# GpSimd's order in a Mamba-2 scan: both exponent additions of the next item ahead of the off-chunk addition

## The reference

```python
seg = cs[:, :, :, None] - cs[:, :, None, :]
lmat = jnp.exp(jnp.where(tri, seg, -jnp.inf))
cb = jnp.einsum('bclgn,bcsgn->bclsg', cc, bc)
y_diag = jnp.einsum('bclsge,bcsgep->bclgep', cb[..., None] * lmat, xdt)
...
y_off = jnp.einsum('bclgn,bcgepn,bclge->bclgep', cc, s_prev, jnp.exp(cs))
return (y_diag + y_off).reshape(b, L, H, P), s_last.reshape(b, H, P, N)
...
y = y_f + y_b[:, ::-1] + d_skip.astype(jnp.float32)[:, None] * xs.astype(jnp.float32)
y = y.reshape(b, L, D_INNER) * jax.nn.silu(z.astype(jnp.float32))
y = rmsnorm(y, g_norm).astype(h.dtype)
```

## Time and profile before

| | |
|---|---|
| time, median of 3 runs | 2935.42 us (2929.05 to 2936.62) |
| span of the profiled execution | 2938.1 us |
| instructions | 47237 |
| PE busy | 2839.0 us, 97% of the span |
| DVE busy | 1724.5 us, 59% |
| ACT busy | 1093.6 us, 37% |
| POOL busy | 260.0 us, 9% |
| part of the span in which items 4 to 19 are worked on | from about 2197 to 2322 us |

### The profile page before, as it was taken

The page is one execution under the profiler, slowest core; times in us unless marked ns, Lnnn a source line. Parts: engine busy times, 40 slices in busy tenths (PEclk is TensorE's granted clock), DMA queues, the critical chain, the costliest instruction groups (busy, mean ns, idle before and its releaser), DMA issues.

```text
span 2938.1 us, 47237 instructions
## 1 busy us (share of the span) xinstructions
PE 2839.0 (97%) x19482; PEld 2689.6 (92%) x19482; DVE 1724.5 (59%) x2584; ACT 1093.6 (37%) x1739; POOL 260.0 (9%) x201
## 2 busy tenths in 40 slices
PE   8999999998799999999999999999989999999998
PEld 6999999986589999999999999999945798999998
DVE  4667666647766655657565536467768747332334
ACT  4111126446865111146211126653324446211124
POOL 0000003000020000011000002000048511000002
PEclk8999999999999999999999999999989999999999
DMA  5445444520044444443443324622221133322233
GB/s 230 138 156 180 152 151 134 159 67 24 23 137 144 149 141 134 151 151 122 163 150 126 115 98 135 186 87 78 67 74 33 58 102 121 115 84 67 73 99 124
DMA packets 102631, 345.21 MB, mean 117 GB/s; under 512 B 10769, under 2 KB 27537, under 8 KB 100881
## 3 DMA queue, kind: packets, MB, share of 16 engines
q1 hardware_dynamic: 96786, 333.15, 34.9%
q10 hardware_dynamic: 5632, 9.05, 0.9%
HBM read 331.54 MB, written 10.62 MB: 116 GB/s over the span
## 4 chain that ended last, share of the span: by engine, by line
PE 83%; DVE 5%; ACT 4%; issue 3%; POOL 2%; DMA 1%; ACTq 0%; DVEq 0%; SPq 0%; POOLq 0%
PE P L1806 78%; ACT pb L946 1%; POOL mraw L707 1%; DVE wl L1187 1%; PE P L1865 1%; POOL toff L711 1%; DMA raw<-wgu_d 1%; DVE xl L1230 0%; DVE st L1320 0%; PE P L2009 0%; PE P L1724 0%; DVE xs L1494 0%; PE P L1750 0%; DVE toff L1529 0%; ACT pb L955 0%
## 5 line engine op out<-in xcount | busy, mean ns | idle before, releaser
L1806 PE MATMUL P<-xh,wh 128*128 128x320 f32 x4016 | 1006.0, 313 | 15.2 <-DVE xl L1230 7.9
L1806 PE MATMUL P<-xl,wh 128*128 128x320 f32 x4016 | 994.0, 310 | 0.0
L1806 PE MATMUL P<-xh,wl 128*128 128x320 f32 x4016 | 993.9, 310 | 0.0
L790 ACT CAST wh<-raw 128x1024 fp32r<-128x1024 f32 (+1 forms) x421 | 471.7, 1121 | 967.7 <-PE P L1806 806.8
L1806 PEld LDWEIGHTS P<-xh,wh 128*128 128x128 f32 x4016 | 693.9, 189 | 33.5 <-issue 14.6
L1187 DVE TENSOR_TENSOR wl<-raw,wh 128x1024 fp32r<-128x1024 f32 (+1 forms) x421 | 552.7, 1313 | 288.5 <-ACT wh L790 288.3
L1806 PEld LDWEIGHTS P<-xl,wh 128*128 128x128 f32 x4016 | 694.3, 189 | 1.2 <-issue 0.4
L1806 PEld LDWEIGHTS P<-xh,wl 128*128 128x128 f32 x4016 | 694.0, 189 | 0.0
L1806 PE MATMUL P<-hh,wh 128*128 128x320 f32 x1408 | 379.4, 310 | 0.0
L1806 PE MATMUL P<-hl,wh 128*128 128x320 f32 x1408 | 377.0, 308 | 0.0
L1806 PE MATMUL P<-hh,wl 128*128 128x320 f32 x1408 | 377.0, 308 | 0.0
(11 more groups left out here) (260 smaller groups left out, 2350.2 us busy)
## 6 DMA issues: line engine op xcount, KB each, us to landing
raw<-wgu_d SPq DMA_DIRECT2D x206, 512.0 KB, 3.7
mraw<-wmod_d SPq DMA_DIRECT2D x128, 512.0 KB, 3.6
raw<-wdB_d SPq DMA_DIRECT2D x64, 704.0 KB, 4.1
raw<-wdA_d SPq DMA_DIRECT2D x32, 704.0 KB, 5.5
raw<-ain_d SPq DMA_DIRECT2D x28, 512.0 KB, 3.6
raw<-sz_d SPq DMA_DIRECT2D x26, 512.0 KB, 3.8
raw<-sx_d SPq DMA_DIRECT2D x24, 512.0 KB, 3.6
raw<-aout_d SPq DMA_DIRECT2D x16, 512.0 KB, 3.6
```

What stands on the lines that cost most here:

```text
L790: nc.scalar.copy(wh[:, u.u % SPLITS, 0:n], raw[:, u.u % 2, 0:n]).then_inc(hi_done, 1)
L1806: ins = nc.tensor.matmul(P[:, u.banks[i], 0:C], w[:, u.u % SPLITS, k * 128:(k + 1) * 128], m[:, k, C * h:C * h + C], start=(k == 0 and w i ...
```

## The change

Within GpSimd's `scan`, `both(nxt, 1)` is issued ahead of `offs(nxt)` where it was issued behind it. For items of chunk 0, which have no `offs`, the order is as it was. No instruction, buffer or semaphore is added or removed, and the other engines' streams are the same.

```diff
                     if nxt < len(ITEMS):
                         both(nxt, 0)
+                        both(nxt, 1)
                         if ITEMS[nxt][0]:
                             offs(nxt)
-                        both(nxt, 1)
                     if i >= 1:
                         squares(i - 1)
```

## The result

The changed kernel takes 2940.95 us (median of 13 runs, 2936.19 to 2945.24), the kernel before 2935.42 us (13 runs, 2928.95 to 2937.99). The ratio is 1.0022, with a 95% interval of 1.0014 to 1.0030: 0.22% slower, some 4 to 9 us. That is a small loss, clear of the measurement's noise. The forecast was 2940.6.

The account below looks back on a forecast made before the run. Scan pace bound by a loop through POOL, DVE and ACT, PE just behind. Terms 4.2 - .3 + 2.1 + .55 - 1.3 = +5.2 us: span 2938.1 to 2943.3, median 2.7 lower, 2940.6; 8 in 10 range 2931.5 to 2947.

Parts of the forecast that it names:

- The lock: DVE's decay product meets `offs`, ends at E (end of the item's second addition) + 1.79; .46 us delay per item with state.
- A step with `blocks`: Steps into items 6, 8, 10, 12, 14, 16: POOL waits for ACT's exponential; 9.00 against 8.31 us, +4.2 in all.
- Plain steps: Steps into items 7, 11, 15, without `blocks` or `btok`: 7.70 against 7.84 us, -.3 in all.
- Steps with `btok` and into 17: Into 9 and 13, POOL's addition starts .16 us ahead of L1499: 8.70, +2.1 together; into 17 8.22, +.55.
- rival B: L1499 goes ahead of POOL's next addition into 9, 13 and 17, each .95 us shorter: +2.3, 2937.7 us; chance .20.
- The last chunk: Steps into items 18 and 19, without states or L1467: 6.6 and 6.1 against 7.25 and 6.72 us, -1.3 for both.
- Items 4 and 5: Start of the reordered items: item 5 keeps its pace, since POOL had spare time there; no term in the sum.
- Behind item 19: After the last item nothing changes: output, splits and first projection follow L1499 at the same distance; no term in the sum.
- what queues behind the new wait: `offs`, squares and `blocks` stand behind the second addition's wait for ACT; only POOL's own chain feels it, priced in the steps.
- Rival C: PE's longer `btok` wait, some 2.1 us, lowers the clock; three chunks lose up to 2.5 us each: 2948.1 us; chance .12.
- Rival A: The loop gains 1.24 us a step until PE's idle time is used up: -6, 2929.4 us; chance .10.

Follow-up runs that it names:

- e3: Changed kernel, with the scan's decay product reading the PSUM sum in place of the old state (its decay left out); 1.0004 of the time before.
- e1: Changed kernel with a second buffer for the second exponential, one for each half; 1.0019 of the time before.
- e9: Changed kernel with two buffers for the second exponential and ACT's square behind the exponentials, profiled once more; 1.0001 of the time before.
- e2: Changed kernel with ACT's second pair of exponentials ahead of its square of the output, one buffer kept; 1.0004 of the time before.
- e10: Changed kernel with POOL's first addition of items 5, 7, 9 and so on waiting until L1499 is ready; 2934.41 us, 1.0008 of before.

## Why the prediction was right

The time (2940.95 against 2940.6) and the sign were right; what counts is whether the terms were.

- *The lock*, that is, a DVE product of two SBUF operands waiting until the POOL operation under way ends. Right. L1467 ends at E + 1.78 (forecast 1.79), L1499 is ready at E + 3.57 (3.57). e3 shows the cause by taking it away.
- *A step with `blocks`, six times.* L700 starts at E + 3.40 (3.41), L1499 ends at E + 5.84 (5.86), the first addition at E + 6.98 (7.02), the second starts at E + 7.69 (7.73). The step is 8.98 against 9.00. The sum of the six is +4.4 with the one of 9.31, against +4.2. The reason given, that the old order hid ACT's turn-round on the one buffer, is only half of it: e1 shows that the buffer alone gives .15, and e9 against e2 that it gives .75 once ACT's square no longer stands in the way. Two waits of almost the same length lie on top of each other, and the text named one.
- *Plain steps, three times.* 7.70, 7.69 and 7.96 against 7.70; they give nothing in place of -.3. The third follows the fall of the clock. And the forecast took 7.84 as the old length of all three, where the one into item 7 was 7.66.
- *Steps with `btok` and into 17.* 8.71 and 8.21 against 8.70 and 8.22, +2.6 against +2.65. L1499 lost the race in all of them; rival B is out, and e10 confirms its price (.97 against .95).
- *The last chunk.* 6.56 and 6.03 against 6.6 and 6.1; -1.4 against -1.3.
- *Items 4 and 5* were taken as unchanged; from E of item 3 to E of item 5 it is .62 less. The clock was below 1.00 in this stretch in both kernels, so how much of it is the change's is open.
- *Behind item 19* was put at nothing, since "nothing is changed" there. That was wrong: +.90, for `offs` of item 19 now stands ahead of the squares that ACT's last square waits for. The passage on what queues behind the new wait had these squares done "a whole step earlier"; behind item 19 there is no further step. The last chunk gains .5 net, not 1.3.
- *Rival C, the clock,* was priced at up to 2.5 us a chunk, with no row behind that figure, and put at .12. It came true in part: PE's wait grew to 2.0 (forecast 2.1), the clock fell once in two such waits, and it cost .6 us (.3 in each of two steps), since PE isn't the engine that sets the pace. The wait was forecast well, but its length alone doesn't decide: 1.53 us was followed by a fall in e3 and 1.97 wasn't. The price was four times too high.
- *Rival A, PE as the bound,* did not come about in the changed kernel. The window of its chunk (item 9's `toff` to item 13's), for the earlier trace rows:

```profile
2232.10:2266.46 34.36, 30.66 (x212) 18.42 (x212) 30.74 (x45) 13.81 (x25) 27.39 (x25) 1.00 0.11 32
```

PE worked as much as before (30.66 against 30.59) in a chunk that took 2.25 us longer; its idle time is 3.7 us (forecast 3.5). Rival A came about in e9.

The sum of the steps from 5 to 19 is +5.62; the forecast terms give +5.25, and the clock's .6 less the .2 of small misses is the rest. With the two ends of the scan it is +5.90, where -.62 and +.90 cancel in part. That the median came out within .4 us of the forecast is partly luck: the interval of the loss runs from 4 to 9 us, and three terms of .6 to .9 (the clock, items 4 and 5, the end) were not in the sum.

## What to carry to other kernels

An operation that seems to be in the way of a critical one may be covering two others: here the off-chunk addition filled the time of a buffer's turn-round, and its new place put it into the path of another engine's product that waits for its end (1.14 us in place of 0.69). Where two loops through several engines are near the same length, count every operation from one fixed event, in both orders; a difference of a sixth of a microsecond in who starts first was worth a whole one. An edit that is worth little alone may be worth far more in a pair (the second buffer, .15 and .75 us a step), so test the pair. And follow the last item by itself: what is covered in the middle of a loop may lie open at its end, as the .90 us here.

## What the runs showed of the hardware

When a DVE product of two SBUF operands waited for a POOL operation and the next POOL operation was already queued, DVE went first in the rows read here: L1499 of the changed kernel ends at 2241.49, and the L707 that was issued at 2240.90 behind L700 takes 1.73 in place of 1.27 us. The waiting product needs .55 us after the release in place of its 0.69. With one operand in PSUM (e3) the product took 0.68 us beside POOL's addition, without a wait.

Waits of PE of almost the same length, 1.97 and 1.99 us in the changed kernel and 1.51 and 1.53 in e3, ended once with the granted clock held at 1.00 (2.4 GHz) and once with it at .50 (1.2 GHz) for some 4 us. Where it fell, the next step with `blocks` was .3 to .8 us longer.
